# Twelve weight rests of the gate projections on GpSimd in place of VectorE

## The reference, cut to what matters

```python
    z = jnp.einsum('btd,dp->btp', h, w_in)
    gq, gk, gv, gg, glr, mq, mk, mv, mo, mgate = jnp.split(z, PROJ_SPLITS, axis=-1)
    ...
    y_gla = rmsnorm(gla_o, gla_g_norm) * jax.nn.silu(gla_gate.astype(f32))
    y_ml = jax.nn.sigmoid(ml_ogate.astype(f32)) * rmsnorm(ml_h, mlstm_g_norm)
```

```python
        rel = jnp.where(tril[:, :, None], bcum[:, :, :, None, :] - bcum[:, :, None, :, :], -jnp.inf)
        scores = jnp.einsum('bhjk,bhik,bhjik->bhji', qc, kc, jnp.exp(rel))
```

## Time and profile before

| | |
|---|---|
| time, median of 3 runs | 2626.37 us (2623.65 to 2626.67) |
| the profiled execution | 2623.75 us, its span 2622.0 us |
| TensorE busy | 2555.5 us, 97% of the span |
| VectorE busy | 1980.2 us, 76% |
| ScalarE busy | 1323.8 us, 50% |
| GpSimd busy | 0.2 us, 4 instructions |
| gate stage | about 414 to 524 us of the span |

### The profile page before, as it was taken

How to read it: one execution, slowest core, us unless ns; L and a number is a source line. 1 busy time by engine, 2 the same in 40 slices (tenths; PEclk the granted TensorE clock), 3 DMA queues, 4 the chain that set the end, 5 groups by cost and what they waited for, 6 DMA issues and landing times.

```text
span 2622.0 us, 41990 instructions
## 1 busy us (share of the span) xinstructions
PE 2555.5 (97%) x16142; PEld 2219.8 (85%) x16142; DVE 1980.2 (76%) x3103; ACT 1323.8 (50%) x1978; POOL 0.2 (0%) x4
## 2 busy tenths in 40 slices
PE   5999999999899999999999999999999999999999
PEld 2687778888788888888888888888888998988888
DVE  4577878868988888888556777777654889567577
ACT  3335335555555555554444544445444654676564
POOL 0000000000000000000000000000000000000000
PEclk8999999999999999999999999999999999999999
DMA  9976675416455555558555555555555445533543
GB/s 399 356 309 265 250 282 206 162 57 257 177 192 192 191 183 187 191 191 311 192 189 184 186 190 192 188 184 188 197 190 185 172 167 180 194 140 118 193 170 134
DMA packets 115939, 530.54 MB, mean 202 GB/s; under 512 B 9856, under 2 KB 10432, under 8 KB 66912
## 3 DMA queue, kind: packets, MB, share of 16 engines
q1 hardware_dynamic: 110448, 507.54, 53.4%
q10 hardware_dynamic: 5360, 21.18, 2.2%
HBM read 526.59 MB, written 2.10 MB: 202 GB/s over the span
## 4 chain that ended last, share of the span: by engine, by line
PE 70%; DVE 8%; ACT 3%; issue 2%; ACTq 0%; DVEq 0%
PE ps L2340 43%; PE ps L2341 22%; DVE lo L1338 3%; ACT hi L639 1%; PE ps L2333 1%; PE ps L2331 1%; PE ps L2332 1%; PE ps L2783 1%; ACT p L1294 0%; DVE R L2061 0%; DVE O L2059 0%; PE ps L2645 0%; PE ps L2642 0%; DVE R L2100 0%; DVE rs L1343 0%
## 5 line engine op out<-in xcount | busy, mean ns | idle before, releaser
L1338 DVE TENSOR_TENSOR lo<-raw,hi 128x1024 fp32r<-128x1024 f32 x700 | 827.7, 1221 | 387.6 <-ACT hi L639 387.3
L639 ACT ACTIVATE hi<-raw 128x1024 fp32r<-128x1024 f32 x700 | 709.0, 1055 | 633.6 <-PE ps L2341 602.6
L2340 PE MATMUL ps<-x,hi 128*128 128x512 f32 x1376 | 330.4, 392 | 5.5 <-DVE x L1854 5.5
L2340 PEld LDWEIGHTS ps<-x,hi 128*128 128x128 f32 x1376 | 253.7, 189 | 55.2 <-issue 5.8
L2340 PE MATMUL ps<-y,hi 128*128 128x512 f32 x1024 | 250.7, 392 | 0.7 <-DVE y L1768 0.6
L2340 PE MATMUL ps<-xp,hi 128*128 128x512 f32 x1024 | 244.7, 391 | 0.1
L2340 PEld LDWEIGHTS ps<-xp,hi 128*128 128x128 f32 x1024 | 188.2, 188 | 36.6 <-ACT hi L639 0.3
L2340 PEld LDWEIGHTS ps<-y,hi 128*128 128x128 f32 x1024 | 186.1, 189 | 35.7 <-issue 1.0
L663 ACT ACTIVATE hi<-raw 128x1024 fp32r<-128x1024 f32 x98 | 102.9, 1058 | 220.5 <-DMA raw<-in_weights 88.3
L2341 PEld LDWEIGHTS ps<-x,lo 128*128 128x128 f32 x1376 | 176.7, 191 | 6.9
L2341 PE MATMUL ps<-x,lo 128*128 128x256 f32 x1376 | 178.8, 283 | 0.0
(11 more groups left out here) (403 smaller groups left out, 4168.6 us busy)
## 6 DMA issues: line engine op xcount, KB each, us to landing
raw<-in_weights SPq DMA_DIRECT2D x453, 1024.0 KB, 4.8
wlast<-in_weights ACTq DMA_DIRECT2D x16, 1024.0 KB, 5.0
spare<-in_weights SPq DMA_DIRECT2D x13, 1024.0 KB, 22.3
over_squares<-in_weights SPq DMA_DIRECT2D x9, 1024.0 KB, 16.8
xf<-in_xt SPq DMA_DIRECT2D x4, 1024.0 KB, 9.6
raw<-in_weights SPq DMA_DIRECT2D x4, 768.0 KB, 4.4
R<-in_xt ACTq DMA_DIRECT2D x1, 2048.0 KB, 7.2
out<-R SPq DMA_DIRECT2D x1, 1024.0 KB, 8.7
```

Of the source, the lines that this page charges most:

```text
L639: act.activation(HI[p % PAIR][:, c], RAW[p % RING][:, c], ACT.Copy).then_inc(hi_ready, 1)
L1338: dve.tensor_tensor(LO[p % PAIR][:, c], RAW[p % RING][:, c], HI[p % PAIR][:, c].bitcast(F32), ALU.subtract).then_inc(lo_ready, 1)
L2340: return pe.matmul(o, h, pair[:, :, k, :], start=start, stop=False, **kw)
```

## The change

The rest of half 1 of gates 2 to 13, twelve halves, is computed by GpSimd instead of VectorE. GpSimd waits for the rounding of its half and for the rest before it (`lo_ready` has to count in order), and VectorE waits, ahead of the half that follows one of GpSimd's, for GpSimd's count.

```diff
--- before.py
+++ after.py
@@ -117,6 +117,7 @@
 FIRST_USE += [(kind, k) for kind, k, half in UNITS if not half and (kind, k) not in FIRST_USE]
 AT = {e: n for n, e in enumerate(FRONT)}
 UNIT = {e: n for n, e in enumerate(UNITS)}
+POOLED = [("gate", k, 1) for k in range(2, 14)]
 ENDS = [UNIT["mod", m[-1], 1] for m in MODS[:4]]
 TURNED = [ENDS[0]] + [u + 1 for u in ENDS[1:]]
 SUMS_AT = 3
@@ -1399,6 +1400,10 @@
                     multiplied_sum(i, k, RAW[HOLDS[t]], (2 * h, 2 * h + 1))
                     return
                 n = HALF[kind, k, h]
+                if (kind, k, h) in POOLED:
+                    return
+                if SPLITS[n - 1] in POOLED:
+                    dve.wait_ge(lo_ready, n)
                 dve.wait_ge(hi_ready, n + 1)
                 dve.tensor_tensor(by_outputs(t, half_of(LO, n)), front_raw(t, h * SLOT // 2, SLOT // 2), by_outputs(t, half_of(HI, n)).bitcast(F32),
                                   ALU.subtract).then_inc(lo_ready, 1)
@@ -2318,6 +2323,15 @@
             after_block(1, ot1, fxh, fxl)
             gated(1, pj1, tail=4)
 
+
+        @block.gpsimd
+        def _(pool):
+            for kind, k, h in POOLED:
+                n, t = HALF[kind, k, h], FIRST_USE.index((kind, k))
+                pool.wait_ge(hi_ready, n + 1)
+                pool.wait_ge(lo_ready, n)
+                pool.tensor_tensor(by_outputs(t, half_of(LO, n)), front_raw(t, h * SLOT // 2, SLOT // 2), by_outputs(t, half_of(HI, n)).bitcast(F32),
+                                   ALU.subtract).then_inc(lo_ready, 1)
 
         @block.tensor
         def _(pe):
```

## The result

The changed kernel takes 2630.32 us (median of 14, 2627.04 to 2631.85), the kernel before beside it 2625.26 us (14, 2623.59 to 2627.53): a ratio of 1.0017, interval [1.0009, 1.0024]. That is slower by 4 to 5 us, within the 0.2% that the prediction called no change, and inside its range (2624 to 2650). It lies 2.0 us above the forecast median, and the profiled run, 2629.2 us with a span of 2627.4, 3.5 us above the forecast of 2625.7. The sum was +1.9; between the two profiles the gate stage is 4.7 us longer and the span 5.4.

A forecast was written before the change was run, and what follows sets the result against it. TensorE, busy 97% of the span, was taken as the bound, its gate-stage pauses being waits for `qk`. Delays at gates 5 to 7 summed to +1.9 us, giving a median of 2628.3 us; range 2624 to 2650 us.

The forecast's parts named there:

- The sum: Gate stage, all places added with a GpSimd operation of 2.3 us: +1.9 us, profiled run 2625.7 us.
- rival A: Gate stage: GpSimd enters after VectorE's single operation under way, between `dec` differences; loop 8.1 us for 6.47; +21 us; chance 0.32.
- What bounds the kernel, and the quiet gates: TensorE busy 97%; gate-stage pauses of 3.8 us from waits for `qk`; quiet gates have 1.8 us of slack, cost 0.
- What goes: Twelve half 1 rests leave VectorE, 13.7 us, mostly cover; at most 1.1 us won, at the second pause.
- Its length: One GpSimd rest of 1,024 columns: taken as 2.3 us, between bounds of 1.23 and 5.1 us.
- D: Assumed duration of one GpSimd rest operation, 2.3 us.
- Its order: VectorE's next half 0 rest waits for GpSimd's half 1 through `lo_ready`: cost 0 up to 3.7 us of operation.
- The way into SBUF: GpSimd and VectorE's two-operand SBUF work exclude each other for whole operations; GpSimd enters only at gaps in VectorE's row.
- Gate 5's half: Before the first pause: GpSimd follows `dec`, ends at 446.45 with `qk` due at 446.35: +0.1 us.
- Gate 6's half: At the second pause: GpSimd enters during the gate sum, `dec` starts at 454.25 instead of 453.18: +1.1 us.
- gate 7's: After the second pause: GpSimd again delays `dec`; scores start at 465.35 for 463.47, +1.9 us including earlier delays.
- What would show it: Profile signs: `qk` wait from 4.4 to about 6.3 us, forecast; `dec` pulled apart or 3 us, rival A.

The follow-up runs named there:

- nine halves alone: Changed kernel with the rests of gates 5, 6 and 7 back on VectorE, the others staying on GpSimd: 2627.56 us, ratio 1.0014 to the kernel before.
- the kernel that only writes: Changed kernel with GpSimd filling its twelve halves with zeros, reading nothing, instead of computing the rest: 2623.81 us, ratio 0.9993 to the kernel before.
- the last experiment: Changed kernel with the rest of half 0 on GpSimd in place of half 1's, same twelve gates: 2638.46 us, ratio 1.0046 to the kernel before.
- gates 5, 6 and 7 only: Changed kernel with only the half 1 rests of gates 5, 6 and 7 on GpSimd: 2630.45 us, ratio 1.0012 to the kernel before.

## Why the prediction was right, and where not

The time lies in the range, and the change is a small one, as forecast. But the kernel is 5.1 us slower by the medians where the sum had 1.9, and the range was as wide as it was in order to reach into rival A, so it says little for the mechanism. The forecast also gave +4.7 for an operation of 3.0 us; that this is near the measured loss is chance, since the operation took 2.4.

**What bounds the kernel, and the quiet gates: right.** The two pauses were the only places that moved, and nine halves alone added no wait.

**What goes: right.** At most 1.1 us, at the second pause: the kernel that only writes has that, 1.61 us of pause for 2.75.

**Its length: right.** D = 2.3 us; the twelve have 2.37 to 2.81, 2.41 in the middle, where the longer ones contain the wait for the VectorE operation under way. VectorE's 1.23 us is half of it. The number was right; its working, ScalarE's time for one operand taken twice and a wait, is a guess that no run tests.

**Its order: right.** No wait of VectorE for `lo_ready` shows in the stage; `lo` rows of VectorE wait for ScalarE's `hi` alone. Where the half that follows comes at once, as with half 0 on GpSimd at 465.46, the order does cost, 2.29 us.

**The way into SBUF: half right, and here is the step that failed.** That the two exclude each other for a whole operation was the value taken and is what the trace shows. That GpSimd "gets in only where VectorE's row of two-operand work has a gap", with the overlap of 0.08 us as the reason, is wrong: at 443.17 and in the last experiment at 419.66 it waits for one operation and then holds up the next in an unbroken row. The overlap of VectorE's own operations did not keep GpSimd out. The turn-taking of rival A, given 0.32, is what the trace shows: GpSimd's operation begins at 443.17, the next `dec` at 443.54, and the `dec` is the one that waits.

**Place by place.** Gate 5's half was priced at +0.1 and is +2.2: GpSimd goes before the second `dec`, not behind it, so the exponential and everything after it slip by a whole operation. Gate 6's half was priced at +1.1 and is +1.0, gate 7's at +0.8 on the scores and is +0.8: there the gate sum left the way free, and both rules say the same. So the sum of +1.9 was short by gate 5's 2.1 us, and by the 0.7 us of the clock, which the text had named as not priced.

**Why A's rule did not give A's +21 us.** Its loop needs half 1 to be rounded before the second `dec` has begun. In the quiet gates of the changed kernel it comes just too late, by 0.15 to 0.4 us where the second `dec` is still under way. One of the closest:

```profile
495.94 0.68 DVE L1470 TENSOR_TENSOR dec<-cum 128x512 f32<-128x512 f32 x1
```

```profile
496.10 2.79 POOL L2333 TENSOR_TENSOR lo<-raw,hi 128x1024 fp32r<-128x1024 f32 x1 [4.45 <-ACT hi L664]
```

GpSimd then waits for the second `dec` and runs beside ScalarE's exponential and copy, under cover; in two quiet gates it still holds back a `qk`, by 0.4 and 0.7 us, inside the slack. The prediction said of A that "once late it stays late"; in the changed kernel the third place ends at 467.5 and the next gate has its cover back. Only with half 0 does a part of that loop come up in the quiet gates. The forecast was nearer the truth than A by its count of places, not by its rule. A's sum has a slip of its own: 8.1 for 6.47 us is 1.6 us a gate, and it counts 1.4 for five of them, 1 us in 21.

**What would show it.** The wait for `qk` was to go from 4.4 to 6.3 us, and it is 6.2; read alone, that would pass for the forecast. It is a coincidence: the chain slipped by 4.1 us, and the low clock behind the first pause turned some of the wait into slow work. The single lengths told it: a `dec` half of 2.89 us right behind one of 0.69 was named as A's mark, and it is there once.

## What to carry to other kernels

Work with two SBUF operands, moved to GpSimd, is no free parallel work beside VectorE operations with two SBUF operands: each such GpSimd operation stops VectorE until it is through, unless VectorE then waits or works from PSUM. Price it at the moment its input gets ready, assuming that it goes in after the single VectorE operation under way, even inside an unbroken row; ask what then stands behind it, and hold it back with a wait until the critical row is through (3 us of 5 here). Before moving work away, look whether it was on the path: 13.7 us of rests were worth 1.1 us. Read the sum of TensorE's waits with its clock beside it, and see whether the profiled execution is a typical one.

## What the runs show of the hardware

- GpSimd's turn comes after one VectorE operation, not after the row (443.17 and 443.54; 419.66 and 419.96). The prediction had it otherwise.
- A GpSimd operation that only writes (0.95 us for 128 x 1024) lengthens no VectorE operation beside it, and VectorE operations with an operand in PSUM keep their 0.42 and 0.45 us beside a GpSimd one that reads (446.88 and 447.22).
- TensorE's clock fell to its lower level behind twelve of the pauses ahead of scores in these profiles, of 1.8 to 3.8 us, and was back 3 to 4 us later, once after more than 6 (460 to 467, gates 5, 6 and 7 only). The next group of scores came 1.4 to 1.7 us later (7.86 and 8.04 us for 6.47), in that case 2.3, where no other wait swallowed it. It did not fall behind any pause of 1.7 us or less, nor behind 2.75 us in the kernel before and 3.20 us in the kernel with gates 5, 6 and 7, while it fell behind 2.74 and 3.20 us in others. What decides that stayed open.
